# Layer norms in the projections' PSUM banks, and a last column chunk that runs block by block

## The chip, the core and the metric

The kernel runs on one core of a Trainium2 chip. The metric is the time of one execution in microseconds (us). The core has TensorE for matrix products (PE in the rows, its weight loads PEld), VectorE (DVE), ScalarE (ACT), GpSimd (POOL) and SyncE (SP), which here only issues DMAs. TensorE writes its sums into PSUM, which has 8 banks of 512 float32 columns on 128 partitions; everything else lives in SBUF.

## The reference

One decoder layer on x, 256 tokens by 2048 columns, all in float32:

```
h  = x @ w_in + b_in                      # 5 x 1024 columns
a  = silu(LN_c(dwconv31(a_val * sigmoid(a_gate))))
s  = sc_b * dwconv3(sc_c * sc_h)
x1 = LN1(ALPHA * x + concat(a, s) @ w_out + b_out)
q  = x1 @ w_q                             # 8 heads x 2 halves x 128
# product keys: the best 16 of 128 per half, the best 16 of 256 pairs, softmax -> gates
f  = (gelu(x1 @ u.T) * gates) @ v         # u, v: 16384 experts x 2048
x2 = LN2(ALPHA * x1 + f)
```

LN is (x - mean) * rsqrt(var + eps) * g + b over the 2048 columns of a token.

## The kernel before

The float32 products are made of three faster ones. Each weight tile is split into a high part (ScalarE rounds it, `hi`, line 457) and the rest (VectorE's `lo`, line 653, or GpSimd's, line 428), and TensorE adds hi*hi, lo*hi and hi*lo. The weights come as 656 units of 128x1024 (512 KB each) through four raw slots and four slots of parts (`RAW`, `SPLIT`). A raw slot is loaded again when the low part of the unit in it is done; ScalarE may write a slot of parts when TensorE has counted the unit four places back as used (`used`). SP and ScalarE run through the units in order, and so do VectorE and TensorE.

The 256 tokens are two blocks of 128, called b = 0 and 1. The 2048 columns are four chunks of 512, d = 0 to 3 (j in the last product). So a layer norm has eight pieces (b, d).

The place of layer norm 1. The out projection `out_units` sums each piece in a bank of its own (`y_banks`). For the last chunk it finishes block 0 first (`y0_done`), then block 1. VectorE adds the residual of a piece (`add_chunk`, line 708), takes its statistics (line 712), and after the last chunk of a block combines them (lines 717 and 719) and gets 1/std with ScalarE's help (line 724). Then it subtracts the mean and multiplies by g (`centre`, line 728), and multiplies by 1/std and adds b (`scale`, line 734). All this is done in place in the SBUF tensor `acc`; ln1_g and ln1_b lie in `xt_raw`. TensorE transposes each finished piece (line 1222), ScalarE and VectorE split it (lines 537 and 741), and after five pieces the first unit of w_q may start (lines 1246 and 1247); three more pieces follow, then the second unit. Over the first four units of w_q, GpSimd makes all low parts.

The place of layer norm 2. The down projection is v, as 32 groups of 4 expert tiles. The last four groups (`LAST`) run column chunk by column chunk: all four groups for j = 0, then for j = 1, and so on, so that VectorE has the sums of a chunk while the next one runs (`add_down`, line 1092). In the last chunk, groups 28 and 29 run for both blocks, and groups 30 and 31 first for block 0 (then `v0_done`), then for block 1. Layer norm 2 works in place in the SBUF tensor `res`. Five of its pieces are centred and scaled by VectorE (`LN2_VECTOR`); three go to ScalarE (lines 628 and 633) and then to GpSimd (lines 445 and 447), which multiplies by g and adds b (`LN2_POOL`).

Each engine's order is written out by hand in its own block; semaphores set the waits.

Of the kernel before, what the change touches and what calls it, by code (L numbers as in the profile page):

```python
# [5 lines left out]
P = 128  # L6
T = 256
# [81 lines left out]
LN2_VECTOR = [(0, 0), (0, 1), (1, 0), (1, 1), (1, 2)]  # L89
LN2_POOL = [(0, 3), (0, 2), (1, 3)]  # L90
# [11 lines left out]
def build(nc, x_t, x_nat, w_in, w_out, w_q, u_w, v_w, params, sub_keys, b_out, ln1_g, ln1_b, ln2_g, ln2_b, out):  # L102
# [11 lines left out]
    with ctx:  # L114
# [94 lines left out]
        for i in (3, 4):  # L209
            c_pairs.append([sb(f"c_hi{i}", [P, GROUP, T], f32r, down2), sb(f"c_lo{i}", [P, GROUP, T], f32r, down2)])  # L210
        down2.close()
        hid = sb("hid", [P, N_KEYS, T], f32)
# [18 lines left out]
        def x1_bank(b, d):  # L231

            return bank[d if b else NCH + d]
# [217 lines left out]
        def _(act):  # L451
            def hi(u, slot_u):

                act.wait_ge(raw_in[slot_u % RAW], 16 // RAW * (u - slot_u % RAW) + 16)
                if not isinstance(u, int) or u >= SPLIT:
                    act.wait_ge(used, USED0 + u - (SPLIT - 1))
                nc.scalar.activation(w_hi[slot_u % SPLIT][:, :], raw[:, slot_u % RAW, :], ACT.Copy).then_inc(hi_done, 1)  # L457
# [84 lines left out]
            def scores_out(t):  # L542
                act.wait_ge(s_ready, t + 1)
                nc.scalar.activation(s_all[:, t, :], bank[2 + t % 2][:, 0:T], ACT.Copy).then_inc(s_copied, 1)

            for t in range(2 * HEADS):
# [7 lines left out]
                nc.scalar.activation(q_t[t % 2][:, :], bank[t % 2][:, 0:T], ACT.Copy).then_inc(qt_done, 1)  # L554
# [66 lines left out]
            for b in range(TB):  # L621
# [5 lines left out]
                for d in mine:  # L627
                    nc.scalar.activation(res[:, b, d * DCH:(d + 1) * DCH], res[:, b, d * DCH:(d + 1) * DCH],
# [14 lines left out]
        def _(dve):  # L643
# [58 lines left out]
            x_at = [acc]  # L702

            def chunk(b, d):
                return x_at[0][:, b, d * DCH:(d + 1) * DCH]

            def add_chunk(b, d, y):
                return link(tt(chunk(b, d), y, chunk(b, d), ALU.add))

            def chunk_stats(b, d, added):  # L710
                dve.wait_ge(ln_chain, added)
                return link(nc.vector.bn_stats(stats[:, b, d, :], chunk(b, d)))
# [18 lines left out]
            def scale(b, d, b_, needs, done):  # L731
# [116 lines left out]
            for d in range(NCH - 1):  # L848
# [3 lines left out]
                added = [add_chunk(b, d, y_banks[d][b]) for b in range(TB)]  # L852
                for b in range(TB):
                    chunk_stats(b, d, added[b])
            stream_lo(lo_next, U_Q + LEAD - lo_next)

            d = NCH - 1
            dve.wait_ge(y0_done, 1)
            chunk_stats(0, d, add_chunk(0, d, y_banks[d][0]))
            moments(0)  # L860
            dve.wait_ge(ln1_in, 32)
            centre(0, 0, ln_g)
            inverse(0, 1)
            c01 = centre(0, 1, ln_g)
            scale(0, 0, ln_b, c01 - 1, x1_done)
            c02 = centre(0, 2, ln_g)
            scale(0, 1, ln_b, c01, x1_done)
            scale(0, 2, ln_b, c02, x1_done)
            dve.wait_ge(used, USED0 + U_Q)
            chunk_stats(1, d, add_chunk(1, d, y_banks[d][1]))  # L870
            moments(1)
            centre(1, 0, ln_g)
            inverse(1, 2)
            c11 = centre(1, 1, ln_g)
            scale(1, 0, ln_b, c11 - 1, x1_done)
            c03 = centre(0, 3, ln_g)
            scale(1, 1, ln_b, c11, x1_done)
            for n in range(X1_HALF):
                x1_lo(n)
            c12 = centre(1, 2, ln_g)  # L880
            scale(0, 3, ln_b, c03, x1_done)
            c13 = centre(1, 3, ln_g)
            scale(1, 2, ln_b, c12, x1_done)
            scale(1, 3, ln_b, c13, x1_done)
# [204 lines left out]
            x_at[0] = res  # L1089

            def add_down(b, d):
                return link(stt(chunk(b, d), chunk(b, d), ALPHA, v_bank(d, b), ALU.mult, ALU.add))

            for u in range(U_DOWN, U_END):
# [7 lines left out]
                if u >= U_LAST and j >= 1 and n < 2 * TB:  # L1102
# [5 lines left out]
                    else:  # L1108
                        chunk_stats(n - TB, j - 1, chain[0])
# [29 lines left out]
        def _(pe):  # L1139
# [90 lines left out]
            def scores(t):  # L1230
# [4 lines left out]
                for b in range(TB):  # L1235
                    i = mm(bank[2 + t % 2][:, b * P:(b + 1) * P], q_t[t % 2][:, b * P:(b + 1) * P],  # L1236
# [182 lines left out]
```

## Time and profile before

| what | value |
|---|---|
| median of 3 runs | 1934.65 us (1933.08 to 1935.37) |
| the profiled execution | 1933.9 us, its span 1932.1 us |
| mean granted TensorE clock | 0.994 |
| PE busy | 1888.9 us (98%) |
| DVE busy | 1283.1 us (66%) |
| ACT busy | 857.9 us (44%) |
| POOL busy | 229.1 us (12%) |

The span is the time from the first to the last instruction; 1.8 us of the execution lie around it. TensorE is busy nearly all the time, so the chain of waits runs through it but for two places: one near 325 to 354 us, between the out projection and w_q, and one after 1918 us, behind the last product. Those two are looked at as timelines, engine by engine. A group of rows with "x4" is four instructions in a row; its length goes from the start of the first to the end of the last. The rows give an instruction's length with the part that overlaps its successor; from start to start a 128x512 operation is some 0.08 us shorter.

### The profile page before, as it was taken

How to read it: one execution, taken by the hardware profiler on the slowest of the kernel's cores; microseconds unless marked ns; L12 is line 12 of the kernel's file. 1: busy time of each engine (PE TensorE's matmuls, PEld its weight loads, DVE VectorE, ACT ScalarE, POOL GpSimd, SP SyncE). 2: the span in 40 equal slices, each digit the busy share in tenths (PEclk: the TensorE clock that was granted, in tenths of full speed). 3: DMA queues.
4: the chain of work that ended last, by engine and by line, in shares of the span. 5: the costliest groups of instructions: out<-in, count | busy, mean ns of one | idle time of the engine just before them, and what ended most of it. 6: DMA issues, size and time to landing. Idle time of an engine off the chain costs nothing.

```text
span 1932.1 us, 34084 instructions
## 1 busy us (share of the span) xinstructions
PE 1888.9 (98%) x12650; PEld 1721.3 (89%) x12650; DVE 1283.1 (66%) x1843; ACT 857.9 (44%) x1084; POOL 229.1 (12%) x101
## 2 busy tenths in 40 slices
PE   8999998899999999999999999999999999999997
PEld 8999977899999999999999999888888888888775
DVE  7999975799947677777777755444444444444555
ACT  5544453344444444444444444444444444444443
POOL 0000025578950000000000000000000000000001
PEclk9999999899999999999999999999999999999999
DMA  7665546455465555555555555655655565555553
GB/s 270 223 210 187 195 162 218 164 175 175 165 205 175 183 176 175 184 174 176 180 178 178 179 182 199 217 188 191 230 185 185 186 191 188 188 191 186 179 185 116
DMA packets 98089, 361.78 MB, mean 187 GB/s; under 512 B 10848, under 2 KB 10976, under 8 KB 96480
## 3 DMA queue, kind: packets, MB, share of 16 engines
q1 hardware_dynamic: 97440, 359.97, 55.6%
q10 hardware_dynamic: 576, 0.96, 0.1%
q8 instruction: 31, 0.51, 0.1%
q14 instruction: 42, 0.34, 0.1%
HBM read 356.69 MB, written 4.19 MB: 187 GB/s over the span
## 4 chain that ended last, share of the span: by engine, by line
PE 94%; DVE 3%; issue 1%; POOL 1%; ACT 1%; DMA 0%; DVEq 0%; POOLq 0%; SPq 0%; ACTq 0%
PE psum L1152 17%; PE psum L1153 17%; PE psum L1154 17%; PE psum L1318 12%; PE psum L1320 12%; PE psum L1319 12%; PE psum L1286 2%; PE psum L1196 1%; PE psum L1198 1%; PE psum L1197 1%; POOL w_lo L428 1%; DVE acc L734 0%; PE psum L1236 0%; DVE acc L728 0%; DMA xt_raw<-in_x_t_dram 0%
## 5 line engine op out<-in xcount | busy, mean ns | idle before, releaser
L457 ACT ACTIVATE w_hi<-raw 128x1024 fp32r<-128x1024 f32 x656 | 695.5, 1061 | 967.4 <-PE psum L1154 492.5
L653 DVE TENSOR_TENSOR w_lo<-raw,w_hi 128x1024 fp32r<-128x1024 f32 x572 | 698.5, 1226 | 486.1 <-ACT w_hi L457 484.6
L1152 PE MATMUL psum<-xt_hi,w_hi 128*128 128x256 f32 x2944 | 828.9, 282 | 15.7 <-DVE xt_lo L667 9.4
L1153 PE MATMUL psum<-xt_lo,w_hi 128*128 128x256 f32 x2944 | 823.8, 280 | 0.0
L1154 PE MATMUL psum<-xt_hi,w_lo 128*128 128x256 f32 x2944 | 823.5, 280 | 0.0
L1152 PEld LDWEIGHTS psum<-xt_hi,w_hi 128*128 128x128 f32 x2944 | 555.6, 189 | 17.7 <-issue 11.7
L1153 PEld LDWEIGHTS psum<-xt_lo,w_hi 128*128 128x128 f32 x2944 | 555.6, 189 | 0.0
L1154 PEld LDWEIGHTS psum<-xt_hi,w_lo 128*128 128x128 f32 x2944 | 555.5, 189 | 0.0
L1318 PE MATMUL psum<-w_hi,c_hi 128*128 128x512 f32 x1024 | 405.3, 396 | 1.8 <-DVE c_lo L1062 1.8
L1320 PE MATMUL psum<-w_hi,c_lo 128*128 128x512 f32 x1024 | 405.0, 396 | 0.0
L1319 PE MATMUL psum<-w_lo,c_hi 128*128 128x512 f32 x1024 | 405.0, 396 | 0.0
L1318 PEld LDWEIGHTS psum<-w_hi,c_hi 128*128 128x128 f32 x1024 | 192.3, 188 | 49.6 <-DVE c_lo L1062 3.2
L1320 PEld LDWEIGHTS psum<-w_hi,c_lo 128*128 128x128 f32 x1024 | 192.4, 188 | 46.6
L1319 PEld LDWEIGHTS psum<-w_lo,c_hi 128*128 128x128 f32 x1024 | 192.4, 188 | 46.4
L428 POOL TENSOR_TENSOR w_lo<-raw,w_hi 128x1024 fp32r<-128x1024 f32 x82 | 213.0, 2612 | 80.1 <-ACT w_hi L457 79.7
L445 POOL TENSOR_TENSOR res<-res,ln2g 128x512 f32<-128x512 f32 x3 | 4.2, 1413 | 1359.4 <-ACT res L633 1359.4
L692 DVE SCALAR_TENSOR_TENSOR cacc<-apad,prm,cacc x232 | 100.9, 476 | 0.0
L1062 DVE TENSOR_TENSOR c_lo<-hid,c_hi 128x1024 fp32r<-128x1024 f32 x32 | 39.2, 1225 | 79.4 <-ACT c_hi L591 79.4
L1196 PE MATMUL psum<-w_hi,mix_hi 128*128 128x512 f32 x128 | 51.0, 399 | 2.3 <-DVE lnt L829 1.3
L1198 PE MATMUL psum<-w_hi,mix_lo 128*128 128x512 f32 x128 | 50.6, 396 | 0.0
L1197 PE MATMUL psum<-w_lo,mix_hi 128*128 128x512 f32 x128 | 50.6, 395 | 0.0
L1035 DVE TENSOR_TENSOR oh2g<-oh2g,gate_t 128x1024 f16<-128x1024 f16 x64 | 44.0, 688 | 1.1
(141 smaller groups left out, 840.1 us busy)
## 6 DMA issues: line engine op xcount, KB each, us to landing
raw<-in_u_w_dram SPq DMA_DIRECT2D x256, 512.0 KB, 3.2
raw<-in_v_w_dram SPq DMA_DIRECT2D x256, 512.0 KB, 3.4
raw<-in_w_in_dram SPq DMA_DIRECT2D x80, 512.0 KB, 3.4
raw<-in_w_out_dram SPq DMA_DIRECT2D x32, 512.0 KB, 3.3
raw<-in_w_q_dram SPq DMA_DIRECT2D x32, 512.0 KB, 3.3
xt_raw<-in_x_t_dram SPq DMA_DIRECT2D x4, 512.0 KB, 8.0
acc<-in_x_nat_dram SPq DMA_DIRECT2D x1, 2048.0 KB, 7.8
x_spill<-acc SPq DMA_DIRECT2D x1, 2048.0 KB, 6.7
```

Of the source, the lines that this page charges most:

```text
L428: nc.gpsimd.tensor_tensor(w_lo[s][:, :], raw[:, s, :], w_hi[s][:, :].bitcast(f32), ALU.subtract).then_inc(lo_done[s], SPLIT)
L457: nc.scalar.activation(w_hi[slot_u % SPLIT][:, :], raw[:, slot_u % RAW, :], ACT.Copy).then_inc(hi_done, 1)
L653: tt(w_lo[slot_u % SPLIT][:, :], raw[:, slot_u % RAW, :], w_hi[slot_u % SPLIT][:, :].bitcast(f32), ALU.subtract).then_inc(lo_done[slot_u % ...
L692: i = stt(s, a, w, s, ALU.mult, ALU.add)
L1152: mm(dst, hi_w[:, sl], xt_hi[:, kk, :], start=st, stop=False)
L1153: mm(dst, hi_w[:, sl], xt_lo[:, kk, :], start=False, stop=False)
L1154: i = mm(dst, lo_w[:, sl], xt_hi[:, kk, :], start=False, stop=en)
L1196: mm(dst, a1, w1, start=st, stop=False)
L1197: mm(dst, a1, w2, start=False, stop=False)
L1318: mm(v_bank(j, b), a1, w1, start=first and h == 0 and e == 0, stop=False)
L1319: mm(v_bank(j, b), a1, w2, start=False, stop=False)
L1320: i = mm(v_bank(j, b), a2, w1, start=False, stop=last and h == 1 and e == 1)
```

## The change

There are four edits.

1. Layer norm 1 keeps its input in PSUM: the residual is added into the bank that holds the projection's sum, statistics and `centre` work there, and `scale` reads the bank and writes `acc` in SBUF. The transposes now write the bank that their piece has left, so the products with w_q and the scores use banks 4 to 7 and no longer 0 to 3.
2. Layer norm 2 does the same in the banks of the down projection; `scale` writes `res`.
3. In the last column chunk all four groups run for block 0, and then all four for block 1. Eight units are then in use at a time, so the last four units get four more slots of parts (`tail_hi`, `tail_lo`), in SBUF that the expert products have left.
4. Of the pieces of layer norm 2, GpSimd keeps one, (1, 3). VectorE does the seven others, the four of block 0 ahead of those of block 1.

```diff
-LN2_VECTOR = [(0, 0), (0, 1), (1, 0), (1, 1), (1, 2)]
-LN2_POOL = [(0, 3), (0, 2), (1, 3)]
+LN2_VECTOR = [(0, 0), (0, 1), (0, 2), (0, 3), (1, 0), (1, 1), (1, 2)]
+LN2_POOL = [(1, 3)]
...
+        def parts_of(u):
+            if isinstance(u, int) and u >= U_END - SPLIT:
+                return tail_hi[u % SPLIT], tail_lo[u % SPLIT]
+            return w_hi[u % SPLIT], w_lo[u % SPLIT]
...
         def x1_bank(b, d):
-            return bank[d if b else NCH + d]
+            return y_banks[d][b]
...
             def hi(u, slot_u):
                 act.wait_ge(raw_in[slot_u % RAW], 16 // RAW * (u - slot_u % RAW) + 16)
-                if not isinstance(u, int) or u >= SPLIT:
+                if isinstance(u, int) and u >= U_END - SPLIT:
+                    act.wait_ge(clo_done, 16)
+                elif not isinstance(u, int) or u >= SPLIT:
                     act.wait_ge(used, USED0 + u - (SPLIT - 1))
...
-                    nc.scalar.activation(res[:, b, d * DCH:(d + 1) * DCH], res[:, b, d * DCH:(d + 1) * DCH],
+                    nc.scalar.activation(res[:, b, d * DCH:(d + 1) * DCH], v_bank(d, b),
                                          ACT.Identity, bias=neg_mean[:, b, :]).then_inc(normed, 1)
...
-            def add_chunk(b, d, y):
-                return link(tt(chunk(b, d), y, chunk(b, d), ALU.add))
+            def add_chunk(b, d):
+                return link(tt(x1_in(b, d), x1_in(b, d), columns(acc, b, d), ALU.add))
...
-            def centre(b, d, g):
-                return link(stt(chunk(b, d), chunk(b, d), mv[:, b, 0:1], g[:, d * DCH:(d + 1) * DCH],
+            def centre(b, d, g, x_in):
+                return link(stt(x_in(b, d), x_in(b, d), mv[:, b, 0:1], g[:, d * DCH:(d + 1) * DCH],
                                 ALU.subtract, ALU.mult))
...
-                stt(chunk(b, d), chunk(b, d), rstd[:, b, :], b_[:, d * DCH:(d + 1) * DCH],
+                stt(columns(x_out, b, d), x_in(b, d), rstd[:, b, :], b_[:, d * DCH:(d + 1) * DCH],
                     ALU.mult, ALU.add).then_inc(done, 1)
...
             def add_down(b, d):
-                return link(stt(chunk(b, d), chunk(b, d), ALPHA, v_bank(d, b), ALU.mult, ALU.add))
+                return link(stt(x2_in(b, d), columns(res, b, d), ALPHA, x2_in(b, d), ALU.mult, ALU.add))
...
-            for j in range(NCH):
-                for g in range(G_LAST, GROUPS - 2 if j == NCH - 1 else GROUPS):
+            for j in range(NCH - 1):
+                for g in range(G_LAST, GROUPS):
...
             for b in range(TB):
-                for g in range(GROUPS - 2, GROUPS):
+                for g in range(G_LAST, GROUPS):
```

How the instructions now stand, at three places.

VectorE in layer norm 1, block 0, from its first `centre` on. Before:

```order
L728 SCALAR_TENSOR_TENSOR acc<-acc,mv,xt_raw 128x512
L724 RECIPROCAL rstd<-rstd 128x1
L728 SCALAR_TENSOR_TENSOR acc<-acc,mv,xt_raw 128x512
L734 SCALAR_TENSOR_TENSOR acc<-acc,rstd,xt_raw 128x512
L728 SCALAR_TENSOR_TENSOR acc<-acc,mv,xt_raw 128x512
L734 SCALAR_TENSOR_TENSOR acc<-acc,rstd,xt_raw 128x512 x2
L708 TENSOR_TENSOR acc<-psum,acc 128x512
```

And now:

```order
L745 SCALAR_TENSOR_TENSOR psum<-psum,mv,xt_raw 128x512
L741 RECIPROCAL rstd<-rstd 128x1
L745 SCALAR_TENSOR_TENSOR psum<-psum,mv,xt_raw 128x512
L751 SCALAR_TENSOR_TENSOR acc<-psum,rstd,xt_raw 128x512
L745 SCALAR_TENSOR_TENSOR psum<-psum,mv,xt_raw 128x512
L751 SCALAR_TENSOR_TENSOR acc<-psum,rstd,xt_raw 128x512 x2
L725 TENSOR_TENSOR psum<-psum,acc 128x512
```

The order is the same; each operation that had two tensors from SBUF now has one from PSUM.

TensorE near the start of the last column chunk (the digit of w_hi is the slot of the unit; a unit has six products per block). Before:

```order
L1318 MATMUL psum<-w_hi0,c_hi0 128x512
L1319 MATMUL psum<-w_lo0,c_hi0 128x512
L1320 MATMUL psum<-w_hi0,c_lo0 128x512
L1318 MATMUL psum<-w_hi0,c_hi0 128x512
L1319 MATMUL psum<-w_lo0,c_hi0 128x512
L1320 MATMUL psum<-w_hi0,c_lo0 128x512
L1318 MATMUL psum<-w_hi1,c_hi0 128x512
```

And now, from the fourth product of the chunk on:

```order
L1350 MATMUL psum<-w_hi0,c_hi0 128x512
L1351 MATMUL psum<-w_lo0,c_hi0 128x512
L1352 MATMUL psum<-w_hi0,c_lo0 128x512
L1350 MATMUL psum<-w_hi1,c_hi0 128x512
L1351 MATMUL psum<-w_lo1,c_hi0 128x512
L1352 MATMUL psum<-w_hi1,c_lo0 128x512
L1350 MATMUL psum<-w_hi1,c_hi0 128x512
```

The second unit now follows after six products of the first, where twelve stood; 96 products are in the chunk as before.

VectorE at the end of layer norm 2's block 0 (`add_down` of block 1 is the last row of each). Before:

```order
L728 SCALAR_TENSOR_TENSOR res<-res,mv,ln2g 128x512
L724 RECIPROCAL rstd<-rstd 128x1
L1119 MEMSET stats 128x1
L734 SCALAR_TENSOR_TENSOR res<-res,rstd,ln2b 128x512
L1092 SCALAR_TENSOR_TENSOR res<-res,psum 128x512
```

And now:

```order
L745 SCALAR_TENSOR_TENSOR psum<-psum,mv,ln2g 128x512
L741 RECIPROCAL rstd<-rstd 128x1
L1140 MEMSET stats 128x1
L745 SCALAR_TENSOR_TENSOR psum<-psum,mv,ln2g 128x512
L751 SCALAR_TENSOR_TENSOR res<-psum,rstd,ln2b 128x512
L745 SCALAR_TENSOR_TENSOR psum<-psum,mv,ln2g 128x512
L751 SCALAR_TENSOR_TENSOR res<-psum,rstd,ln2b 128x512
L745 SCALAR_TENSOR_TENSOR psum<-psum,mv,ln2g 128x512
L751 SCALAR_TENSOR_TENSOR res<-psum,rstd,ln2b 128x512 x2
L1113 SCALAR_TENSOR_TENSOR psum<-res,psum 128x512
```

All eight passes over block 0 now stand ahead of block 1, where two stood; behind block 1's mean there are six passes, where eight stood.

## Rows read from the trace of the kernel before

**Rows 1.** The page: the chain that ended last, shares by engine.
```profile
PE 94%; DVE 3%; issue 1%; POOL 1%; ACT 1%; DMA 0%; DVEq 0%; POOLq 0%; SPq 0%; ACTq 0%
```

**Rows 2.** The chain in order of time: start, length, what.
```profile
341.10 0.66 DVE acc L734
...
346.18 0.55 PE psum L1152
...
354.04 0.39 PE psum L1152
...
1918.32 0.25 PE psum L1320
```

**Rows 3.** Timeline of VectorE, layer norm 1: start, length, instruction, [idle before].
```profile
329.24 2.89 DVE L728 SCALAR_TENSOR_TENSOR acc<-acc,mv,xt_raw 128x512 f32<-128x512 f32 x1
332.05 5.57 DVE L734 SCALAR_TENSOR_TENSOR acc<-acc,rstd,xt_raw 128x512 f32<-128x512 f32 x2
337.54 0.68 DVE L708 TENSOR_TENSOR acc<-psum,acc 128x512 f32<-128x512 f32 x1
...
339.35 1.02 DVE L728 SCALAR_TENSOR_TENSOR acc<-acc,mv,xt_raw 128x512 f32<-128x512 f32 x1
```

**Rows 4.** Timeline of GpSimd, the same stretch.
```profile
328.61 11.22 POOL L428 TENSOR_TENSOR w_lo<-raw,w_hi 128x1024 fp32r<-128x1024 f32 x4 [5.17 <-ACT w_hi L457]
```

**Rows 5.** Timeline of TensorE, the same stretch.
```profile
330.54 0.39 PE L1198 MATMUL psum<-w_hi,mix_lo 128*128 128x512 f32 x1
...
350.84 1.47 PE L1222 MATMUL psum<-ident,acc 128*128 128x128 f32 x12
```

**Rows 6.** Windows: busy PE, PEld, DVE, ACT, POOL; granted clock; DMA share, GB/s.
```profile
335.00:337.00 2.00, 0.58 (x4) 0.34 (x4) 2.00 (x1) 0.00 (x0) 2.00 (x1) 0.86 0.72 229
...
349.00:351.00 2.00, 2.00 (x15) 2.00 (x14) 0.39 (x1) 0.00 (x0) 0.00 (x0) 0.73 0.38 160
```

**Rows 7.** Timeline of VectorE, the first layer norm over channels.
```profile
262.01 2.28 DVE L823 TENSOR_TENSOR cacc<-cacc,psum 128x2048 f32<-128x2048 f32 x1
```

**Rows 8.** Timeline of GpSimd, beside it.
```profile
261.44 2.93 POOL L435 TENSOR_TENSOR w_lo<-raw,w_hi 128x1024 fp32r<-128x1024 f32 x1 [2.74 <-ACT w_hi L457]
```

**Rows 9.** Groups by line and shape: busy us, mean ns, idle before.
```profile
L785 DVE SCALAR_TENSOR_TENSOR sct<-scpad,prm,sct 128x256 f32<-128x256 f32 x16 | 7.6, 476 | 0.0
L567 ACT ACTIVATE hid<-psum 128x256 f32<-128x256 f32 x20 | 7.3, 367 | 0.0
...
L567 ACT ACTIVATE psum<-psum 128x256 f32<-128x256 f32 x15 | 5.5, 368 | 0.0
...
L778 DVE SCALAR_TENSOR_TENSOR scpad<-psum,prm,hval 128x256 f32<-128x256 f32 x8 | 3.8, 479 | 4.9 <-issue 2.5 <-ACT hval L497 2.4
```

**Rows 10.** Timeline of VectorE, the last chunk and layer norm 2.
```profile
1897.41 1.23 DVE L653 TENSOR_TENSOR w_lo<-raw,w_hi 128x1024 fp32r<-128x1024 f32 x1 [1.57 <-ACT w_hi L457]
1898.55 0.68 DVE L1092 SCALAR_TENSOR_TENSOR res<-res,psum 128x512 f32<-128x512 f32 x1
...
1912.99 0.69 DVE L1092 SCALAR_TENSOR_TENSOR res<-res,psum 128x512 f32<-128x512 f32 x1 [3.15 <-PE psum L1320]
...
1920.41 0.94 DVE L728 SCALAR_TENSOR_TENSOR res<-res,mv,ln2g 128x512 f32<-128x512 f32 x1
...
1922.95 1.75 DVE L734 SCALAR_TENSOR_TENSOR res<-res,rstd,ln2b 128x512 f32<-128x512 f32 x1
...
1927.61 1.40 DVE L734 SCALAR_TENSOR_TENSOR res<-res,rstd,ln2b 128x512 f32<-128x512 f32 x2
```

**Rows 11.** Timeline of GpSimd, layer norm 2.
```profile
1918.31 1.27 POOL L447 TENSOR_TENSOR res<-res,ln2b 128x512 f32<-128x512 f32 x1
...
1922.47 1.68 POOL L445 TENSOR_TENSOR res<-res,ln2g 128x512 f32<-128x512 f32 x1
1924.22 1.59 POOL L447 TENSOR_TENSOR res<-res,ln2b 128x512 f32<-128x512 f32 x1
```

**Rows 12.** The page: DMA issues, us to landing.
```profile
raw<-in_v_w_dram SPq DMA_DIRECT2D x256, 512.0 KB, 3.4
```

More of the change, by code:

```diff
@@ L210, in build @@
             c_pairs.append([sb(f"c_hi{i}", [P, GROUP, T], f32r, down2), sb(f"c_lo{i}", [P, GROUP, T], f32r, down2)])
+        tail_hi = [sb(f"tail_hi{i}", [P, HALF * P], f32r, down2) for i in range(SPLIT)]
+        tail_lo = [sb(f"tail_lo{i}", [P, HALF * P], f32r, down2) for i in range(SPLIT)]
         down2.close()
+        def parts_of(u):
+            if isinstance(u, int) and u >= U_END - SPLIT:
+                return tail_hi[u % SPLIT], tail_lo[u % SPLIT]
+            return w_hi[u % SPLIT], w_lo[u % SPLIT]
         hid = sb("hid", [P, N_KEYS, T], f32)
@@ L851, in _, with centre1, scale1 @@
                 dve.wait_ge(used, USED0 + U_OUT + 4 * (NCH + d + 1))
-                added = [add_chunk(b, d, y_banks[d][b]) for b in range(TB)]
+                added = [add_chunk(b, d) for b in range(TB)]
                 for b in range(TB):
-                    chunk_stats(b, d, added[b])
+                    chunk_stats(b, d, added[b], x1_in)
             stream_lo(lo_next, U_Q + LEAD - lo_next)
+            def centre1(b, d):
+                return centre(b, d, ln_g, x1_in)
+            def scale1(b, d, needs):
+                scale(b, d, ln_b, needs, x1_done, x1_in, acc)
             d = NCH - 1
             dve.wait_ge(y0_done, 1)
-            chunk_stats(0, d, add_chunk(0, d, y_banks[d][0]))
+            chunk_stats(0, d, add_chunk(0, d), x1_in)
             moments(0)
             dve.wait_ge(ln1_in, 32)
-            centre(0, 0, ln_g)
+            c00 = centre1(0, 0)
             inverse(0, 1)
[L864 to L868, printed above, removed]
+            c01 = centre1(0, 1)
+            scale1(0, 0, c01 - 1)
+            c02 = centre1(0, 2)
+            scale1(0, 1, c01)
+            scale1(0, 2, c02)
             dve.wait_ge(used, USED0 + U_Q)
-            chunk_stats(1, d, add_chunk(1, d, y_banks[d][1]))
+            chunk_stats(1, d, add_chunk(1, d), x1_in)
             moments(1)
-            centre(1, 0, ln_g)
+            c10 = centre1(1, 0)
             inverse(1, 2)
[L874 to L877, printed above, removed]
+            c11 = centre1(1, 1)
+            scale1(1, 0, c11 - 1)
+            c03 = centre1(0, 3)
+            scale1(1, 1, c11)
             for n in range(X1_HALF):
                 x1_lo(n)
[L880 to L884, printed above, removed]
+            c12 = centre1(1, 2)
+            scale1(0, 3, c03)
+            c13 = centre1(1, 3)
+            scale1(1, 2, c12)
+            scale1(1, 3, c13)
             for n in range(X1_HALF, TB * NCH):
@@ L1246, in _ @@
             pe.wait_ge(x1lo_done, X1_HALF)
-            stationary_unit(U_Q, U_Q, 0, bank[0][:, 0:T])
+            stationary_unit(U_Q, U_Q, 0, bank[4][:, 0:T])
             for n in range(X1_HALF, TB * NCH):
@@ L1250, in _ @@
             pe.wait_ge(x1lo_done, 8)
-            stationary_unit(U_Q + 1, U_Q + 1, 1, bank[0][:, 0:T])
+            stationary_unit(U_Q + 1, U_Q + 1, 1, bank[4][:, 0:T])
             for t in range(1, 2 * HEADS):
@@ L1311, in down @@
                 wait_lo(pe, u, ur)
[L1312 removed]
+                hi_w, lo_w = parts_of(ur)
                 for e in range(2):
```

76 lines of the change are left out of this document (43 added, 33 removed).

## Prediction

> **What bounds the kernel.** I read the shares of the chain of waits first: 94% of it is TensorE, 3% VectorE [rows 1]. A change to the layer norms can therefore pay in two places only, where the chain leaves TensorE. The chain in order of time names them: between the out projection and w_q, and behind the last product, which ends at 1918.57 us [rows 2]. Then I read each engine's timeline there.
>
> In the first place the out projection is over at 330.54 + 0.39 = 330.93 us [rows 5], but VectorE adds the last chunk of block 1 only at 337.54 [rows 3]. In between stand three passes over block 0, of 2.89 us and of 5.57 us for two, where a pass elsewhere takes 0.66 us from start to start [rows 2, 3]. All that time GpSimd makes four low parts, from 328.61 to 339.83 [rows 4]. Each of the slow passes reads two tensors from SBUF, and so does GpSimd. So I take it that they hold each other up. The first product with w_q starts at 346.18 and the second unit at 354.04 [rows 2].
>
> In the second place eight passes stand behind block 1's mean, and while GpSimd works on its pieces they take up to 1.75 us each [rows 10, 11]. The last ends at 1927.61 + 1.40 = 1929.01 us; its store and the end of the span at 1932.1 follow 3.1 us later.
>
> **Edit 1, layer norm 1 in PSUM.** The order is the same; only the operands move. Does VectorE still wait for GpSimd when one of its two inputs is in PSUM? The trace has that case once: line 823 (one input SBUF, one PSUM, 2048 wide) takes 2.28 us from 262.01, wholly inside a GpSimd low part that runs to 264.37 [rows 7, 8]. That is no longer than a 1024-wide operation of 1.23 us, doubled [rows 10]. So I take the hold as gone. The sum, from start to start:
> - The three slow passes: 337.54 - 329.24 = 8.30 us before, 3 x 0.66 = 1.98 now. Saved 6.32 us. Block 1's addition would start at 331.22, and the product it waits for is over at 330.93, so no new wait comes up, by 0.3 us.
> - Block 1's first pass took 1.02 us beside GpSimd [rows 3], now about 0.74. Saved 0.28 us.
> - All that stands behind it on VectorE (two more centres and two scales, a late centre of block 0, five low parts of x1) moves up unchanged. w_q starts at about 339.6 instead of 346.18: 6.6 us.
> - Is something else late then? GpSimd, no longer held, needs 4 x 2.4 us (the 2.93 us of line 435 less the 0.57 it stood still until 262.01 [rows 7, 8]) from 328.61, so it ends at 338.2; the first unit of w_q needs only the first of the four. The transposes of block 0's pieces come while TensorE has nothing else. They hide.
> - From w_q's first unit to the second, 354.04 - 346.18 = 7.9 us pass: 24 products, 12 transposes, ScalarE and VectorE. I leave that as it is.
>
> What does an operation of VectorE cost that reads PSUM and writes PSUM? Reading: line 778 with a PSUM input takes 479 ns, line 785 with none 476 ns [rows 9]. So nothing. The Trainium skill says otherwise ("VectorE: DVE Perf Modes", section on the TRN2 errata): a fixed part of 58 cycles from SBUF and 120 from PSUM, which at the page's 0.96 GHz is 65 ns more per operation. By that, an estimate, the thirteen passes and additions before w_q and the five of block 1 at the end would give back 1.2 us. This case's rows 9 don't show it. I go by the rows.
>
> Writing PSUM: no operation of VectorE does it before. The nearest row is ScalarE's gelu, 367 ns into SBUF and 368 ns into PSUM [rows 9]. So the lower bound is nothing. The upper one is that an operation which reads and writes the same bank streams twice: half of the 1.05 us that lie between a 2048-wide operation (2.28) and a 1024-wide one (1.23), 0.52 us each [rows 7, 10]. I take nothing, as the nearest row has it, and keep 0.52.
>
> The banks 4 to 7 for w_q and the scores are a renaming: each is written after the low part of the piece in it is done. I cost it at nothing.
>
> **Edits 2 and 4, layer norm 2.** Block 1's mean is there as before, and the first pass starts at 1920.41 [rows 10]. Now six passes follow instead of eight, on VectorE alone: 6 x 0.66 us and 0.2 us for the reciprocal, and the last one's end 0.08 us later, so 1924.65 us instead of 1929.01: 4.4 us. What is late next? GpSimd keeps piece (1, 3). It starts at 1922.47 and took 1.68 + 1.59 us beside VectorE; alone, 1.27 us a pass [rows 11], with 0.1 us between. So it ends at about 1925.1. That now ends last, and the 3.1 us of the store follow. Saved: 1929.01 - 1925.1 = 3.9 us. The two extra pieces of block 0 go to VectorE, which idled before 1918.57.
>
> **Edit 3, the last chunk.** 96 products of 0.233 us are the same 22.4 us, from about 1896.1 on. Block 0 is complete at their half, 1907.3 us, where it was at 1912.99 [rows 10]. Its eight passes then take from 1907.3 + 1.8 (addition, statistics, mean) to about 1914.7, well before block 1's sum at 1918.57. In the old order (5.6 us of room) they would not have fitted. So this edit is what hides edit 4's extra passes; by itself it gains nothing.
>
> Its price: for block 0 a unit lasts 1.4 us on TensorE instead of 2.8, so eight units must be split in 11.2 us. Who is late? The last unit's raw tile is loaded once the low part begun at 1897.41 is done, 1898.6, plus 3.4 us [rows 10, 12]: there at 1902.0, and ScalarE has it ready at 1903.1. VectorE is the tighter one: from 1897.41 it does four low parts of 1.14 us (1898.55 - 1897.41), two additions of 0.60 and two statistics of 0.65 ahead of the last low part [rows 10], so that one ends at 1897.41 + 7.06 + 1.23 = 1905.7 us. TensorE wants it at 1896.1 + 7 x 1.4 = 1905.9. The margin is 0.2 us, so I charge 0.1 us. Each 0.1 us that an addition or a statistic takes longer in PSUM costs 0.4 us here.
>
> **The sum.** 6.6 + 3.9 - 0.1 = 10.4 us off the span of 1932.1: 1921.7, and with the 1.8 us around it 1923.5 for the profiled execution, which was 0.75 us below the median of the runs. From the median: 1934.65 - 10.4 = 1924.2 us.
>
> **The rivals.**
> - *The clock stays up.* The granted clock fell from 2.4 to 1.2 GHz at about 336.4 us (0.86 over 335 to 337), after TensorE had stood mostly idle since 331, and came back at about 349.9 (0.73 over 349 to 351), 3.8 us after w_q began [rows 6]. Now the pause ends at 339.6. If the clock stays up, w_q's first unit takes 24 x 0.117 = 2.8 us instead of 4.7, and VectorE's last five passes (to 342.8) set the transposes; the second unit would start at 344.8 instead of 347.4. That is 2.6 us more: 1921.6 us. Against it: the idle stretch from 331 to the fall is still there. A pause that falls otherwise may also cost up to 2 us.
> - *A bank read and written by one operation is slow*, 0.52 us each: eight such operations stand before w_q (4.2 us), four behind the last product (2.1 us, and there VectorE then ends last, so 1.6 net of the 0.5 by which it ended first), and two ahead of the last low part (1.0). Gain 10.4 - 6.8 = 3.6 us: 1931.0 us. Against it: rows 9, for another engine and two banks.
> - *The hold stays.* VectorE and GpSimd block each other also with one SBUF input. Then nothing is gained before w_q, and at the end about 2.5 us: 1932.1 us. Against it: rows 7 and 8. The Trainium skill ("SBUF — State Buffer", Who interferes with whom) says the shared ports are an exclusive lock, taken by VectorE operations with two SBUF inputs; by it this rival falls.
> - *TensorE starves in the last chunk.* If the last four units still come every 2.8 us (a load later than its slot, say), TensorE waits up to 4 x 1.4 = 5.6 us: 1929.8 us. For it: the margin of 0.2 us.
> - *Slower than before.* The in-place operations in PSUM cost more than a second stream. The fourteen of them on the path decide from 10.4 / 14 = 0.74 us extra each; at 1.3 us extra, three times their length, the kernel takes 1934.65 - 10.4 + 18.2 = 1942 us. No row speaks for it; none shows the operation either.
>
> **How the numbers follow.** The forecast has 0.60, the clock 0.15, the slow bank 0.09, the hold 0.05, the starving 0.08, the slower case 0.03. The range of 1921.0 to 1928.5 takes in the forecast with 1 us of spread between runs, the clock, a part of the starving, and some 0.3 us per in-place operation; it leaves out the hold and the slow bank in full. A change within 0.2% (3.9 us) can't be told from none. Faster by more, below 1930.8: forecast, clock, starving, and a third of the slow bank, 0.86. Within it: the hold, the rest of the slow bank, 0.11. Slower: 0.03.
>
> **What would show it.** In the changed profile: the passes of layer norm 1 beside GpSimd's low parts at 0.74 us each, GpSimd's four low parts at 2.4 us, w_q's start at 339 to 340 us, block 0's addition in layer norm 2 at 1907 on the old clock of times (11.2 us before the last product's end), the last VectorE pass 6.1 us behind that end, and GpSimd's as the last piece. In-place passes over 0.9 us, or a pause of TensorE between the last chunk's units above 0.3 us, would prove the forecast wrong in that step.

## The result

The changed kernel takes 1924.76 us (median of 6 runs, 1922.98 to 1925.66), the kernel before 1935.06 us (6 runs, 1933.08 to 1937.05). The ratio is 0.9948, with an interval of 0.9939 to 0.9958. That is 10.3 us by the medians and 10.1 us by the ratio; 10.4 us was forecast. Two executions in the later rounds, one of the kernel before (4278 us) and one of the repeated change (6714 us), were slow ones, and the ratios leave them out.

| what | before | after |
|---|---|---|
| the profiled execution | 1933.9 us | 1925.22 us |
| its span | 1932.1 us | 1923.4 us |
| mean granted TensorE clock | 0.994 | 0.996 |
| DVE busy | 1283.1 us | 1276.0 us |
| POOL busy | 229.1 us | 221.1 us |

The two spans differ by 8.7 us only. The reason lies ahead of the part that got faster. The addition that begins the last part of layer norm 1 (block 0, last chunk) comes at 325.37 us before and at 326.95 us after. It waits for TensorE for 3.1 us in both traces, so the earlier additions and statistics, which edit 1 moved into PSUM too, don't set it. The changed program run again has it at 325.02, and in the eleven traces of this study it lies anywhere from 324.1 to 327.0. So I measure all further times from that addition and call it the mark. 8.7 + 1.6 = 10.3 us is then what the change gave in these two traces.

**Layer norm 1.** The timeline of VectorE in the profile after (start, length, instruction, [idle before]); these rows answer to [rows 3]:

```profile
326.95 0.70 DVE L725 TENSOR_TENSOR psum<-psum,acc 128x512 f32<-128x512 f32 x1 [3.11 <-PE psum L1230]
...
330.82 0.75 DVE L745 SCALAR_TENSOR_TENSOR psum<-psum,mv,xt_raw 128x512 f32<-128x512 f32 x1
331.48 1.40 DVE L751 SCALAR_TENSOR_TENSOR acc<-psum,rstd,xt_raw 128x512 f32<-128x512 f32 x2
332.80 0.69 DVE L725 TENSOR_TENSOR psum<-psum,acc 128x512 f32<-128x512 f32 x1
...
334.62 0.75 DVE L745 SCALAR_TENSOR_TENSOR psum<-psum,mv,xt_raw 128x512 f32<-128x512 f32 x1
```

GpSimd's timeline of the same stretch, which answers to [rows 4]:

```profile
330.20 9.36 POOL L437 TENSOR_TENSOR w_lo<-raw,w_hi 128x1024 fp32r<-128x1024 f32 x4 [5.19 <-ACT w_hi L468]
```

The three passes over block 0 that took 8.30 us take 332.80 - 330.82 = 1.98 us, wholly beside GpSimd's low parts. GpSimd needs 9.36 us for its four where it needed 11.22. Neither engine holds the other up any more.

**TensorE behind it.** Its timeline, which answers to [rows 2, 5]:

```profile
332.35 1.47 PE L1254 MATMUL psum<-ident,acc 128*128 128x128 f32 x12
...
341.15 0.55 PE L1184 MATMUL psum<-xt_hi,w_hi 128*128 128x256 f32 x1 [2.16 <-issue]
...
349.10 0.39 PE L1184 MATMUL psum<-xt_hi,w_hi 128*128 128x256 f32 x1 [1.74 <-DVE xt_lo L758]
```

The twelve transposes in the first row are those of block 0's first three pieces. w_q starts 14.20 us behind the mark, where it was 346.18 - 325.37 = 20.81: 6.6 us earlier. The second unit is 6.5 us earlier (22.15 instead of 28.67). The windows (busy PE, PEld, DVE, ACT, POOL; granted clock; DMA share, GB/s) show that the clock still falls, as in [rows 6]:

```profile
337.00:339.00 2.00, 1.33 (x8) 0.69 (x6) 2.00 (x4) 0.60 (x1) 2.00 (x2) 0.85 0.67 213
339.00:341.00 2.00, 0.00 (x0) 0.00 (x0) 2.00 (x5) 0.60 (x1) 0.56 (x1) 0.50 0.66 242
...
345.00:347.00 2.00, 2.00 (x19) 2.00 (x19) 0.00 (x0) 0.47 (x1) 0.00 (x0) 0.94 0.95 393
```

It falls to 1.2 GHz at about 338.4 us, 2.8 us before w_q's first product, and is back at about 345.2, 4.1 us behind it.

**The last chunk and layer norm 2.** VectorE's timeline, which answers to [rows 10]:

```profile
1899.45 1.21 DVE L665 TENSOR_TENSOR tail_lo<-raw,tail_hi 128x1024 fp32r<-128x1024 f32 x1
1902.38 0.69 DVE L1113 SCALAR_TENSOR_TENSOR psum<-res,psum 128x512 f32<-128x512 f32 x1 [1.72 <-PE psum L1352]
...
1908.36 1.40 DVE L751 SCALAR_TENSOR_TENSOR res<-psum,rstd,ln2b 128x512 f32<-128x512 f32 x2
1913.45 0.69 DVE L1113 SCALAR_TENSOR_TENSOR psum<-res,psum 128x512 f32<-128x512 f32 x1 [3.68 <-PE psum L1352]
...
1918.11 1.40 DVE L751 SCALAR_TENSOR_TENSOR res<-psum,rstd,ln2b 128x512 f32<-128x512 f32 x2
```

The chain of waits there (start, length, what):

```profile
1900.70 0.23 PE psum L1352
1900.92 0.29 PE psum L1350
1901.21 0.23 PE psum L1351
```

And GpSimd's timeline, which answers to [rows 11]:

```profile
1917.42 1.27 POOL L454 TENSOR_TENSOR res<-res,ln2g 128x512 f32<-128x512 f32 x1 [1364.85 <-ACT res L644]
1918.77 1.26 POOL L456 TENSOR_TENSOR res<-res,ln2b 128x512 f32<-128x512 f32 x1
```

Block 0 is complete 1913.42 - 1902.38 = 11.04 us before the last product ends, its passes are done at 1909.76, and behind the last product VectorE needs 1919.51 - 1913.42 = 6.09 us and GpSimd 6.6 us. The last low part ends at 1900.66, and in the chain one product behind it takes 0.29 us instead of 0.23: the split came 0.06 us late. From the last product to the end of the span it is 10.0 us, where it was 1932.1 - 1918.57 = 13.5.

### The profile page after: what moved, and what is told of

The parts are those of the page before. It is cut to its first block, busy times and chain, and to the rows that moved or that the text cites. A ratio compares the mean times of both kernels' runs of the same rounds, so it can differ in the third digit from the quotient of the medians.

```text
span 1923.4 us, 34079 instructions
## 1 busy us (share of the span) xinstructions
PE 1888.8 (98%) x12650; PEld 1722.1 (90%) x12650; DVE 1276.0 (66%) x1847; ACT 854.6 (44%) x1080; POOL 221.1 (11%) x97
## 4 chain that ended last, share of the span: by engine, by line
PE 95%; DVE 2%; issue 1%; POOL 1%; ACT 1%; DMA 0%; POOLq 0%; DVEq 0%; SPq 0%; ACTq 0%
PE psum L1184 18%; PE psum L1185 18%; PE psum L1186 17%; PE psum L1350 12%; PE psum L1351 12%; PE psum L1352 12%; PE psum L1318 2%; PE psum L1228 1%; PE psum L1230 1%; PE psum L1229 1%; POOL w_lo L437 1%; PE psum L1268 0%; DMA xt_raw<-in_x_t_dram 0%; DVE cacc L831 0%; DVE psum L745 0%
## 5 line engine op out<-in xcount | busy, mean ns | idle before, releaser
L1350 PE MATMUL psum<-w_hi,c_hi 128*128 128x512 f32 x1008 | 399.0, 396 | 1.8 <-DVE c_lo L1085 1.8
L1352 PE MATMUL psum<-w_hi,c_lo 128*128 128x512 f32 x1008 | 398.7, 396 | 0.0
L1351 PE MATMUL psum<-w_lo,c_hi 128*128 128x512 f32 x1008 | 398.7, 396 | 0.0
```

The source lines that it names most:

```text
L1350: mm(v_bank(j, b), a1, w1, start=first and h == 0 and e == 0, stop=False)
L1351: mm(v_bank(j, b), a1, w2, start=False, stop=False)
L1352: i = mm(v_bank(j, b), a2, w1, start=False, stop=last and h == 1 and e == 1)
```

## The experiments

All marks are read from the profiled executions. "Mark" is the start of block 0's last addition in layer norm 1; the ratios are to the kernel before in the same rounds, with 95% intervals. Each mark comes from one trace. The diffs show the main lines of each edit; `...` stands for what is left out.

| kernel | mark to w_q | mark to second unit | mark to last product's end | from there to the span's end | median us | ratio |
|---|---|---|---|---|---|---|
| before | 20.81 | 28.67 | 1593.2 | 13.5 | 1935.06 | |
| after | 14.20 | 22.15 | 1586.5 | 10.0 | 1924.76 | 0.9948 (0.9939 to 0.9958) |
| ln1_alone | 14.20 | 23.04 | 1587.9 | 13.5 | 1927.11 | 0.9967 (0.9954 to 0.9979) |
| ln2_alone | 20.82 | 29.22 | 1593.6 | 10.0 | 1930.22 | 0.9982 (0.9973 to 0.9992) |
| chunk_alone | 20.82 | 29.58 | 1593.9 | 12.5 | 1932.53 | 0.9993 (0.9983 to 1.0002) |
| old_chunk | 14.19 | 22.70 | 1587.0 | 11.8 | 1925.24 | 0.9957 (0.9940 to 0.9973) |
| scale_sbuf | 18.99 | 26.73 | 1591.4 | 10.0 | 1928.00 | 0.9970 (0.9961 to 0.9980) |
| pool_waits | 14.21 | 25.61 | 1592.7 | 13.5 | 1934.00 | 1.0000 (0.9990 to 1.0010) |
| reorder | 12.94 | 21.24 | 1585.6 | 10.0 | 1922.38 | 0.9949 (0.9937 to 0.9961) |
| changed_again | 14.19 | 22.80 | 1587.1 | 10.0 | 1924.44 | 0.9952 (0.9939 to 0.9964) |
| interleave | 13.08 | | 1583.3 | 10.0 | 1920.37 | 0.9924 (0.9911 to 0.9938) |

In interleave another unit stands between w_q's first and second, so that cell is left empty. The medians of before beside them: 1933.93 us for the first four experiments, 1933.88 for the next four, 1934.69 for the last.

### Edit 1 alone (ln1_alone)

The kernel after, with layer norm 2 and the last chunk as before:

```diff
-LN2_VECTOR = [(0, 0), (0, 1), (0, 2), (0, 3), (1, 0), (1, 1), (1, 2)]
-LN2_POOL = [(1, 3)]
+LN2_VECTOR = [(0, 0), (0, 1), (1, 0), (1, 1), (1, 2)]
+LN2_POOL = [(0, 3), (0, 2), (1, 3)]
...
 def x2_in(b, d):
-    return v_bank(d, b)
+    return res[:, b, d * DCH:(d + 1) * DCH]
...
-            for j in range(NCH - 1):
-                for g in range(G_LAST, GROUPS):
+            for j in range(NCH):
+                for g in range(G_LAST, GROUPS - 2 if j == NCH - 1 else GROUPS):
...
```

> Edit 1 alone: layer norm 1 in PSUM, layer norm 2 and the last chunk as before. Theory (VectorE and GpSimd hold each other up only where VectorE reads two tensors from SBUF): from the addition of block 0's last piece to the first product with w_q 14.2 us instead of 20.8, and 6.6 us off the time, a ratio to the kernel before of 0.9966. Rival (the gain of the whole change came from layer norm 2 and the last chunk): ratio near 1.000.

Measured: w_q starts 14.20 us behind the mark, as in the whole change, and the tail is 13.5 us, as before. The median fell by 6.8 us. The second unit gained only 28.67 - 23.04 = 5.6 us. Here the clock was back 6.0 us behind w_q's first product (0.63 over 344 to 345 us) instead of 4.1; the 1.9 us more at half the clock cost 0.9 us. The section on the prediction returns to that.

### Edits 2, 3 and 4 alone (ln2_alone)

Layer norm 1 stays in SBUF, layer norm 2 and the last chunk are those of after:

```diff
 def x1_in(b, d):
-    return y_banks[d][b]
+    return acc[:, b, d * DCH:(d + 1) * DCH]
...
```

> Edits 2, 3 and 4 without edit 1: layer norm 1 in SBUF as before. Theory: from the last product's end to the end of the span 10.0 us as in the changed kernel instead of 13.5, and 3.5 to 3.8 us off the time, ratio 0.9981; layer norm 1 with its passes of 2.8 us as before. If the two parts help each other (an earlier start of w_q that the rest then loses), the ratio would be another than that of the whole change divided by that of edit 1 alone.

VectorE's timeline of this kernel in layer norm 1 still has the held passes, as [rows 3]:

```profile
328.49 2.89 DVE L745 SCALAR_TENSOR_TENSOR acc<-acc,mv,xt_raw 128x512 f32<-128x512 f32 x1
331.31 5.58 DVE L751 SCALAR_TENSOR_TENSOR acc<-acc,rstd,xt_raw 128x512 f32<-128x512 f32 x2
```

The tail has its 10.0 us. The two parts multiply to 0.9967 x 0.9982 = 0.9949, the whole has 0.9948. So nothing is left over beyond what the intervals, 2 to 3 us to either side for the two together, would hide.

### Edit 3 alone (chunk_alone)

The kernel before, with the last chunk's loop order and its own tiles for the parts:

```diff
-for j in range(NCH):
-    for g in range(G_LAST, GROUPS - 2 if j == NCH - 1 else GROUPS):
+for j in range(NCH - 1):
+    for g in range(G_LAST, GROUPS):
...
 for b in range(TB):
-    for g in range(GROUPS - 2, GROUPS):
+    for g in range(G_LAST, GROUPS):
...
```

> Edit 3 alone: the last column chunk runs block 0 over all four groups and then block 1, with the four more slots of parts; both layer norms in SBUF, three pieces for GpSimd. The forecast's step: by itself this gains nothing, so 13.5 us from the last product's end to the end of the span, ratio 1.000. Rival: GpSimd's passes over block 0's two pieces come 5.6 us earlier, and only its two passes over piece (1, 3) then hold up VectorE behind the last product, so the last VectorE pass ends about 1 us sooner and the span behind the last product is about 12.5 us, ratio 0.9995.

GpSimd's timeline of this kernel, the first and the last of its passes over block 0 and those over block 1:

```profile
1911.11 1.29 POOL L453 TENSOR_TENSOR res<-res,ln2g 128x512 f32<-128x512 f32 x1 [1353.74 <-ACT res L643]
...
1915.10 1.29 POOL L455 TENSOR_TENSOR res<-res,ln2b 128x512 f32<-128x512 f32 x1
1922.10 1.33 POOL L453 TENSOR_TENSOR res<-res,ln2g 128x512 f32<-128x512 f32 x1 [5.72 <-ACT res L643]
1923.51 1.59 POOL L455 TENSOR_TENSOR res<-res,ln2b 128x512 f32<-128x512 f32 x1
```

GpSimd's work on block 0 is over at 1916.4, 1.8 us before the last product ends (1918.20), where in [rows 11] it reached into layer norm 2 of block 1. Two of VectorE's passes still take 1.75 us beside its work on block 1. So the edit by itself shortens the tail from 13.5 to 12.5 us, as this experiment's rival had it; the forecast's step had 13.5. In the runs (0.9993, up to 1.0002) that can't be told from nothing.

### The change without edit 3 (old_chunk)

The other way round: the kernel after, with the last chunk's loops as before.

```diff
-for j in range(NCH - 1):
-    for g in range(G_LAST, GROUPS):
+for j in range(NCH):
+    for g in range(G_LAST, GROUPS - 2 if j == NCH - 1 else GROUPS):
...
 for b in range(TB):
-    for g in range(G_LAST, GROUPS):
+    for g in range(GROUPS - 2, GROUPS):
```

> The changed kernel without edit 3: in the last chunk, groups 28 and 29 run for both blocks as before, with edits 1, 2 and 4 kept. Theory (edit 3 is what hides the extra passes of block 0): the eight passes of block 0 end about 1.8 us after the last product, block 1's mean and all behind it come 1.8 us later, and from the last product's end to the end of the span it is 11.8 us instead of 10.0; ratio to the kernel before 0.9957. Rival (block 0's passes find room in any case): 10.0 us and 0.9947.

VectorE's timeline, block 0's last two passes and block 1's addition:

```profile
1911.95 1.40 DVE L751 SCALAR_TENSOR_TENSOR res<-psum,rstd,ln2b 128x512 f32<-128x512 f32 x2
1913.27 0.69 DVE L1113 SCALAR_TENSOR_TENSOR psum<-res,psum 128x512 f32<-128x512 f32 x1
```

The last product ends at 1911.38, but VectorE comes to block 1's addition 1.9 us later, from block 0's passes, with no idle time between. The tail is 11.8 us instead of 10.0. Edit 3 is therefore worth 1.8 us beside edit 4, and it does hide the extra passes. The medians (1925.24 and 1924.76, from different rounds) are too close to show it.

### One operand back in SBUF (scale_sbuf)

The claim that carries 6.6 of the 10.4 us is that the hold needs two inputs in SBUF. Here `centre` reads the bank and writes `acc`, so that `scale` reads two tensors in SBUF; nothing else changes. If the bank itself, and not the number of SBUF inputs, were what helps, `centre` would be the slow one as well.

```diff
 def centre1(b, d):
-    return centre(b, d, ln_g, x1_in)
+    return link(stt(columns(acc, b, d), x1_in(b, d), mv[:, b, 0:1], ln_g[:, d * DCH:(d + 1) * DCH],
+                    ALU.subtract, ALU.mult))
 def scale1(b, d, needs):
-    scale(b, d, ln_b, needs, x1_done, x1_in, acc)
+    scale(b, d, ln_b, needs, x1_done, lambda b, d: columns(acc, b, d), acc)
```

> The changed kernel with one half of edit 1 undone: in layer norm 1, centre reads the bank and writes acc, and scale reads acc and ln1_b, both in SBUF. Centre then has one input from SBUF, scale two. Theory (two SBUF inputs make the hold): beside GpSimd's four low parts the centres still take 0.75 us and the scales 2 to 2.8 us each; block 1's addition comes 2 to 4 us later than in the changed kernel (5.85 us behind block 0's addition there), and so does w_q. Rival (what counts is that the output of centre stays in PSUM, or that VectorE writes SBUF less): centres slow down as well, or scales don't.

VectorE's timeline:

```profile
327.95 0.74 DVE L875 SCALAR_TENSOR_TENSOR acc<-psum,mv,xt_raw 128x512 f32<-128x512 f32 x1
328.62 4.98 DVE L751 SCALAR_TENSOR_TENSOR acc<-acc,rstd,xt_raw 128x512 f32<-128x512 f32 x2
...
336.07 0.73 DVE L875 SCALAR_TENSOR_TENSOR acc<-psum,mv,xt_raw 128x512 f32<-128x512 f32 x1
336.72 1.94 DVE L751 SCALAR_TENSOR_TENSOR acc<-acc,rstd,xt_raw 128x512 f32<-128x512 f32 x1
```

And GpSimd's:

```profile
327.33 10.78 POOL L437 TENSOR_TENSOR w_lo<-raw,w_hi 128x1024 fp32r<-128x1024 f32 x4 [5.19 <-ACT w_hi L468]
```

Inside the same 10.78 us of GpSimd the passes with one SBUF input take 0.74 us and the two of 4.98 us together, with two, take 2.2 and 2.8 us. That settles it: the number of SBUF inputs decides. Block 1's addition comes 3.6 us later than in the change, within the 2 to 4 us expected; w_q comes 4.8 us later, more than that, since block 1's first scale pass is held too (1.94 us). The second unit comes 4.6 us later than in the change, and the median is 3.6 us higher than that of the repeated change in the same rounds (1928.00 and 1924.44). The Trainium skill ("SBUF — State Buffer", Who interferes with whom) describes the same thing as an exclusive lock between the two engines, taken by VectorE operations with two SBUF inputs; these rows agree.

### GpSimd waits instead (pool_waits)

The same hold can be avoided without PSUM, if GpSimd keeps still meanwhile. The kernel before, with one line ahead of GpSimd's low parts of w_q:

```diff
+pool.wait_ge(x1_done, X1_HALF)
```

> The kernel before with one wait more: GpSimd begins the low parts of w_q only when five pieces of layer norm 1 are scaled. The operands of VectorE are those of before, two from SBUF. Theory (it is GpSimd that holds these passes): the passes ahead of w_q all take 0.74 us, the addition of block 1 comes 5.85 us behind that of block 0 instead of 12.2, and the first product with w_q starts 14.2 us behind it; then the last passes of layer norm 1 meet GpSimd's low parts and the second unit loses 2 to 4 us of that. Rival (the passes are slow because of the weight and ln1 loads that land in SBUF, or for being SBUF passes at all): they take up to 2.9 us as before, with GpSimd idle.

VectorE's timeline, then GpSimd's:

```profile
330.18 0.75 DVE L729 SCALAR_TENSOR_TENSOR acc<-acc,mv,xt_raw 128x512 f32<-128x512 f32 x1
330.85 1.40 DVE L735 SCALAR_TENSOR_TENSOR acc<-acc,rstd,xt_raw 128x512 f32<-128x512 f32 x2
...
342.87 2.86 DVE L735 SCALAR_TENSOR_TENSOR acc<-acc,rstd,xt_raw 128x512 f32<-128x512 f32 x1
345.65 2.83 DVE L729 SCALAR_TENSOR_TENSOR acc<-acc,mv,xt_raw 128x512 f32<-128x512 f32 x1
```

```profile
337.73 10.20 POOL L428 TENSOR_TENSOR w_lo<-raw,w_hi 128x1024 fp32r<-128x1024 f32 x4 [13.35 <-DVE acc L735]
```

With GpSimd still, the passes with all operands in SBUF take 0.75 us, as those in PSUM do: the bank brings nothing but the absence of the hold. w_q starts 14.21 us behind the mark, the gain of edit 1. But now GpSimd's four low parts meet the three last passes, which take 2.6 to 2.9 us, and the second unit comes at 25.61: 3.1 us of the 6.6 are left. At the last product only 0.5 us of them are left (1592.7 instead of 1593.2). The windows show where:

```profile
345.00:347.00 2.00, 0.66 (x4) 0.42 (x4) 2.00 (x2) 0.52 (x1) 2.00 (x2) 1.00 0.35 133
347.00:349.00 2.00, 0.00 (x0) 0.00 (x0) 2.00 (x2) 0.07 (x1) 0.93 (x1) 1.00 0.55 205
349.00:351.00 2.00, 1.31 (x8) 0.84 (x8) 1.89 (x4) 1.04 (x2) 0.00 (x0) 0.86 0.85 279
351.00:353.00 2.00, 1.08 (x5) 1.08 (x6) 1.07 (x3) 1.09 (x2) 0.76 (x1) 0.50 1.07 438
```

TensorE stood idle again ahead of the second unit, but for some transposes, and the clock fell a second time. The second unit, from 351.92 us, ran at 1.2 GHz: its 24 products came every 0.213 us instead of 0.117, which costs 2.3 us. The runs give 1.0000 (0.9990 to 1.0010): a start 6.6 us earlier was worth nothing that they can show.

### Less ahead of w_q, and the change again (reorder, changed_again)

In the change one centre pass of block 0 and the fifth low part of x1 still stand ahead of w_q. Here the pass goes behind the low parts, and TensorE waits for four low parts instead of five, in an order that puts (0, 2) last:

```diff
-c03 = centre1(0, 3)
 scale1(1, 1, c11)
-for n in range(X1_HALF):
+for n in (0, 1, 3, 4, 2):
     x1_lo(n)
+c03 = centre1(0, 3)
...
-pe.wait_ge(x1lo_done, X1_HALF)
+pe.wait_ge(x1lo_done, X1_HALF - 1)
```

> The changed kernel with two operations of VectorE moved behind the four low parts of x1 that w_q's first unit reads: the centre of piece (0, 3), and the low part of (0, 2). Theory (VectorE's work from block 1's addition on sets the start of w_q, and the first unit of w_q hides 4.7 us of it): w_q starts 1.26 us sooner after block 0's addition (12.9 us instead of 14.2), the second unit as much sooner, and the time is 1.2 us below the changed kernel's, ratio to the kernel before 0.9942. Rival (the transposes or ScalarE's high parts set the start): no gain, or the second unit keeps its place.

> The changed kernel itself, beside the others on the same chip. Expected: ratio 0.9948 to the kernel before, as in the first comparison, and about 0.0006 above the reordered one.

w_q starts 12.94 us behind the mark instead of 14.19, as expected, and the last product ends 1.5 us earlier than in the repeated change, 0.9 earlier than in its first trace. The medians, in the same rounds, are 2.1 us apart (1922.38 and 1924.44), but the ratios differ by 0.0003 only (0.9942 was expected), and the intervals cover each other: the gain is seen in the traces and not shown by the runs. The repeated change gives 0.9952 (0.9939 to 0.9964), close to the first 0.9948. Its second unit starts at 22.80, 0.65 us later than in the first trace, because the clock came back later. The window of the repeated change in which it did:

```profile
344.00:345.00 1.00, 1.00 (x8) 1.00 (x7) 0.00 (x0) 0.00 (x0) 0.00 (x0) 0.62 1.06 434
```

That is at about 344.8 us, 5.6 us behind w_q's first product (339.21), where it was 4.1 in the first trace.

### A unit that fills the pause (interleave)

Between the first and the second unit of w_q TensorE stands idle for some 1.7 us, waiting for the second half of x1. The first half of the next head's columns needs only what is there already. Beside the order of the last experiment, that unit is put in between, into a bank of its own (`count` is by how much a unit raises `used`):

```diff
 for n in range(X1_HALF, TB * NCH):
     transpose_x1(n)
+stationary_unit(U_Q + 2, U_Q + 2, 0, bank[5][:, 0:T], count=0)
 pe.wait_ge(x1lo_done, 8)
-stationary_unit(U_Q + 1, U_Q + 1, 1, bank[4][:, 0:T])
-for t in range(1, 2 * HEADS):
+stationary_unit(U_Q + 1, U_Q + 1, 1, bank[4][:, 0:T], count=2)
+stationary_unit(U_Q + 3, U_Q + 3, 1, bank[5][:, 0:T])
+scores(0)
+for t in range(2, 2 * HEADS):
...
```

> The reordered kernel with TensorE taking w_q's third unit (first half of the second key half) between its first and second: the third unit reads only the four pieces of x1 that are there, and fills the time in which the last three pieces are split. Theory (between the 12 transposes and the second unit TensorE idles 1.7 us, only for the high and low parts of the last pieces): the third unit's 2.8 us cover that idle time, all behind it comes 1.7 us sooner, and the time is 1.7 us below the reordered kernel's, ratio to the kernel before 0.993. Rival (the low parts of later w_q units, 2.4 us each on GpSimd, or the copies for the scores become late because units are now used faster): the idle time turns up again within the next units, and nothing is gained.

TensorE's timeline and its waits from 320 to 470 us (for what; total, times, longest):

```profile
344.53 1.47 PE L1255 MATMUL psum<-ident,acc 128*128 128x128 f32 x12
345.76 0.36 PE L1184 MATMUL psum<-xt_hi,w_hi 128*128 128x256 f32 x1
```

```profile
PE psum L1255 <- DVE acc L751: 3.0, 1, 3.0
PE psum L1184 <- issue: 1.5, 1, 1.5
```

In reorder the same list had one row more:

```profile
PE psum L1184 <- DVE xt_lo L758: 1.7, 1, 1.7
```

The wait for the second half is gone. From the mark to the last product it is 1583.3 us, 2.3 less than in reorder; 1.7 were expected, and the clock, back 4.1 us behind w_q's first product instead of 4.9, accounts for 0.4. The median is 1920.37 us. Its interval (0.9911 to 0.9938) lies just below that of the change in its first rounds (0.9939 to 0.9958), and touches that of reorder (0.9937 to 0.9961). So this version beats the kernel before by 14.3 us in the same rounds and, in other rounds, the change; what the filling unit adds by itself rests on the traces.

## Why the prediction was right

The forecast was 1924.2 us; 1924.76 was measured, and the mechanism was the one forecast. That the gain came within 0.1 us of the sum is partly luck: the interval of the ratio allows 8.1 to 11.8 us, and of the sum's two parts one gave 0.2 us more than forecast and the other 0.35 us less. Step by step:

- **The slow passes** (6.32 us forecast): 8.30 - 1.98 = 6.32 us measured. scale_sbuf shows that the two SBUF inputs are the cause, which the prediction had inferred from one operation [rows 7, 8]; pool_waits shows that GpSimd is what holds them.
- **w_q** was forecast 6.6 us earlier and is 6.6 us earlier. GpSimd's four low parts were put at 9.6 us and took 9.36.
- **Reading and writing one bank** was taken as nothing. An in-place pass takes 0.75 us, one in SBUF with GpSimd still 0.75 (pool_waits), and the next starts after 0.66 us in both. From the mark to w_q it is 14.20 us in the change and 14.21 in pool_waits, which does the same passes in SBUF. The rival of a slow bank (0.52 us each) is out. The Trainium skill ("VectorE: DVE Perf Modes", TRN2 errata) has a fixed part of 58 cycles from SBUF and 120 from PSUM, 65 ns more at its 0.96 GHz, by an estimate. No row here shows it, neither in the length nor from start to start. (The prediction counts five operations at the end for it; behind the last product stand seven.)
- **From the first to the second unit** I left the 7.9 us as they were. It is 7.95 us in this trace, but 8.84 in ln1_alone and 8.6 in changed_again. The clock came back 4.1 us behind w_q's first product in the change and 5.6 us in its repetition, which is the same program. In the kernel before it is 7.86 us, but 8.40 and 8.76 in ln2_alone and chunk_alone, which have the same layer norm 1. So this term has a spread of about 1 us, which the prediction took in only with its 1 us between runs, and the two traces compared both happen to lie at its low end. Over the traces with the old and the new layer norm 1 and no other change there (three and four), the last product's end moves from 1593.6 to 1587.1 us behind the mark, 6.4 us.
- **The clock** was given 0.15 to stay up. It fell in every trace. In the kernel before it was back at 350.1 us (0.73 over 349 to 351), 3.9 us behind w_q's first product; the prediction reads 349.9 and 3.8 from that row. The second fall in pool_waits is what it meant by a pause that falls otherwise.
- **The last chunk**: block 0 complete 11.2 us before the end of the products (11.04 measured); a late split charged with 0.1 us (0.06 measured). TensorE did not starve.
- **The products of the last chunk** were taken at 0.233 us each, as before. The 48 that read the new slots `tail_hi` and `tail_lo` come every 0.227 us, the other 48 every 0.233, in all four traces with edit 3 that were compared (the change, its repetition, ln2_alone and chunk_alone), and old_chunk, which has the slots, shows the same. That is 0.3 us which nobody forecast; no run shows why. It is why 6.7 us are gained up to the last product, where the second unit gained 6.5.
- **Behind the last product**: VectorE's end forecast at 6.1 us and measured at 6.09, GpSimd's at 6.5 and measured at 6.6. The mis-sized term is the store: the 3.1 us were read from a store on SP's queue, while the last piece is GpSimd's and its store goes by ScalarE's queue, at 1923.4 - 1920.03 = 3.4 us. Whether that queue makes it longer, or the store that SP issued 0.5 us before, is open: in the kernel before three stores on ScalarE's queue landed in 2.5 us (median). The part gave 3.5 us where 3.9 was forecast.
- **"By itself it gains nothing"**, said of edit 3, is wrong by 1.0 us of the profile: it takes GpSimd's work on block 0 out of layer norm 2 of block 1 (chunk_alone). It does not enter the sum, since edit 4 removes that work altogether.

The sum measured is 6.7 us up to the last product (6.5 forecast) and 3.55 behind it (3.9 forecast), 10.3 us. By medians the two groups of edits alone gave 6.8 and 3.7 us.

## What to carry to other kernels

When VectorE passes take several times their usual length at one place only, look what GpSimd does there and count the SBUF inputs of both: one input in PSUM ended the hold at no cost. Delaying GpSimd ended it there too, but moved it to the next passes, and that with a second fall of the clock left 0.5 us of 6.6. And an engine's earlier start is worth only what the next wait leaves: filling a pause of the bounding engine with work whose inputs were ready gave some 2 us in the traces, on top of shortening the chain ahead of it.

## What the runs showed of the hardware

- The hold works both ways. Beside held passes GpSimd's 128x1024 subtraction takes 11.22 / 4 = 2.80 us, beside the scale passes alone (scale_sbuf) 10.78 / 4 = 2.70, beside passes with one SBUF input 9.36 / 4 = 2.34. A held pass takes up to 2.9 us, near the length of one such subtraction.
- The granted clock fell from 2.4 to 1.2 GHz in every trace ahead of w_q: in the kernel before at 336.4 us, when TensorE had done eight transposes since the out projection, and in the change at 338.4, amid the last four of twenty. It was back 4.1 us behind w_q's first product in the change and 5.6 us in the same program run again; the eleven traces have 3.1 us (pool_waits) to 6.0 us (ln1_alone).
- The same 128x512 product comes every 0.227 us when its weights lie in the four new slots, and every 0.233 us when they lie in the old ones (24 products from 1891.08 to 1896.68 us in the change). The cause is open.
- The moment at which block 0's last addition starts scatters: 326.95 and 325.02 us for two executions of the same program, over 2.9 us in all traces. A difference of two spans is better read from a mark behind that point.
- A 256 KB store of the result landed 2.5 us after its issue on SP's queue in both kernels (median of five and of seven). On ScalarE's it took 2.5 us before (median of three) and 3.0 us in the change, which has one store there, as in the six other kernels with one.
